# A two-network kernel on one core: head norms summed side by side on TensorE, and products reordered where stages join

## The reference

```python
def rms_norm(x, gain):
    y = x32 * lax.rsqrt(jnp.mean(x32 * x32, axis=-1, keepdims=True) + EPS)
    return (y * gain).astype(x.dtype)

def fox_attention(h, norm_g, w_in, b_f, q_gain, k_gain, w_out):
    xn = rms_norm(h, norm_g)
    q, k, v, f_logit, o_gate = jnp.split(xn @ w_in, [D, 2 * D, 3 * D, 3 * D + H], axis=-1)
    q = rms_norm(q.reshape(B, L, H, hd), q_gain) * (hd ** -0.5)
    k = rms_norm(k.reshape(B, L, H, hd), k_gain)
    ...  # softmax over q.k plus the forget sums, times v: o
    o = o * jax.nn.sigmoid(o_gate)
    return o @ w_out

# second block, the mixer's end
merged = jax.nn.sigmoid(ga) * (ya @ w_branch_sb) + jax.nn.sigmoid(gd) * (yd @ w_branch_da)
return merged @ w_out
```

## Time and profile before

| | |
|---|---|
| median of 3 runs | 1312.75 us (1312.34 to 1313.7) |
| the profiled execution's own time | 1312.96 us |
| its span, first to last instruction | 1311.3 us |
| mean granted TensorE clock | 0.999 |
| busy: PE, PEld, DVE, ACT, POOL | 99%, 96%, 73%, 48%, 5% |
| read from HBM | 250.27 MB, 192 GB/s over the span |
| share of the chain that ended last | PE 84%, DVE 7%, ACT 4%, DMA 3%, issue 2% |

### The profile page before, as it was taken

One profiled execution on the slowest core, in us unless ns is written; L12 is line 12 of the kernel. 1 busy time (PEld: TensorE's weight loads), 2 busy tenths in 40 slices (PEclk: granted clock), 3 DMA queues, 4 the chain that ended last, 5 costly groups with the idle time before them and its releaser, 6 DMA issues.

```text
span 1311.3 us, 27391 instructions
## 1 busy us (share of the span) xinstructions
PE 1295.7 (99%) x11118; PEld 1256.6 (96%) x11118; DVE 955.5 (73%) x1245; ACT 629.6 (48%) x740; POOL 62.0 (5%) x102
## 2 busy tenths in 40 slices
PE   9999999999999999999999999999999999999998
PEld 9998799999999899999999999999999899999986
DVE  7666688888567766788875788766967667877744
ACT  6365554434354345544443544443545674644433
POOL 2000000000002000000000000000011000000000
PEclk9999999999999999999999999999999999999999
DMA  8541256666745333566676587676476335476543
GB/s 290 193 156 52 103 206 204 213 194 222 240 162 207 124 121 131 208 199 204 217 242 227 179 284 263 227 242 238 152 264 208 123 138 174 162 230 221 189 164 124
DMA packets 40404, 252.30 MB, mean 192 GB/s; under 512 B 4544, under 2 KB 4800, under 8 KB 16144
## 3 DMA queue, kind: packets, MB, share of 16 engines
q1 hardware_dynamic: 29232, 211.89, 46.8%
q0 software_dynamic: 10816, 39.32, 9.5%
q10 hardware_dynamic: 288, 0.13, 0.0%
HBM read 250.27 MB, written 1.05 MB: 192 GB/s over the span
## 4 chain that ended last, share of the span: by engine, by line
PE 84%; DVE 7%; ACT 4%; DMA 3%; issue 2%; DVEq 0%; ACTq 0%; SPq 0%
PE ps L2199 68%; PE ps L2864 4%; DVE w_lo L1110 3%; ACT w_hi L486 2%; DMA raw<-in_units_mix_in 2%; DMA raw<-in_units_ffn_up 1%; PE ps L2317 1%; PE ps L2219 1%; PE ps L2548 1%; PE ps L2425 1%; PE ps L2597 1%; PE ps L2358 1%; PE ps L2651 1%; ACT scratch L697 1%; DVE proj L1550 0%
## 5 line engine op out<-in xcount | busy, mean ns | idle before, releaser
L2199 PE MATMUL ps<-x_hi,w_hi 128*128 128x258 f32 (+2 forms) x2016 | 578.2, 287 | 2.5 <-DVE x_lo L1264 1.4
L2199 PE MATMUL ps<-x_hi,w_lo 128*128 128x258 f32 (+2 forms) x2016 | 572.9, 284 | 0.0
L486 ACT ACTIVATE w_hi<-raw 128x2048 fp32r<-128x2048 f32 (+1 forms) x178 | 352.6, 1981 | 424.8 <-PE ps L2199 323.9
L2199 PE MATMUL ps<-x_lo,w_hi 128*128 128x258 f32 (+2 forms) x1856 | 527.7, 284 | 0.0
L1110 DVE TENSOR_TENSOR w_lo<-raw,w_hi 128x2048 fp32r<-128x2048 f32 (+1 forms) x178 | 422.5, 2373 | 127.5 <-ACT w_hi L486 126.4
L2199 PEld LDWEIGHTS ps<-x_hi,w_hi 128*128 128x128 f32 x2016 | 380.8, 189 | 7.0 <-DVE x_lo L1264 2.2
L2199 PEld LDWEIGHTS ps<-x_hi,w_lo 128*128 128x128 f32 x2016 | 381.2, 189 | 0.0
L2199 PEld LDWEIGHTS ps<-x_lo,w_hi 128*128 128x128 f32 x1856 | 350.4, 189 | 0.3
L2199 PE MATMUL ps<-g_hi,w_lo 128*128 128x256 f32 (+1 forms) x576 | 162.8, 283 | 0.0
L2199 PE MATMUL ps<-g_hi,w_hi 128*128 128x256 f32 (+1 forms) x576 | 162.8, 283 | 0.0
L2199 PE MATMUL ps<-g_lo,w_hi 128*128 128x256 f32 (+1 forms) x576 | 162.2, 282 | 0.0
(11 more groups left out here) (387 smaller groups left out, 1631.2 us busy)
## 6 DMA issues: line engine op xcount, KB each, us to landing
raw<-in_units_ffn_up SPq DMA_DIRECT2D x44, 1024.0 KB, 4.9
raw<-in_units_glu_up SPq DMA_DIRECT2D x44, 1024.0 KB, 5.1
v_tok<-in_w_ada_t POOLq DMA_DIRECT2D x72, 512.0 KB, 4.0
raw<-in_units_ffn_down SPq DMA_DIRECT2D x16, 1408.0 KB, 6.1
raw<-in_units_mix_in SPq DMA_DIRECT2D x20, 1024.0 KB, 5.2
raw<-in_units_hgrn_in SPq DMA_DIRECT2D x16, 1024.0 KB, 4.9
raw<-in_units_fox_in SPq DMA_DIRECT2D x14, 1024.0 KB, 4.9
raw<-in_units_glu_down SPq DMA_DIRECT2D x8, 1408.0 KB, 6.1
```

What stands on the lines that cost most here:

```text
L486: nc.scalar.activation(w_hi[s][:, 0:size], raw[s][:, 0:size], ACT.Copy).then_inc(hi_ready, 1)
L2199: ins = T_.matmul(dst, fixed, moving, start=(kt == 0 and i == 0), stop=(kt == kts - 1 and i == 2))
```

## The change

1. **Head sums.** Each of the four sums of a group has only 32 output rows now (16 equal rows for each of a tile's two heads), and the four stand side by side in bank 4. ACT takes the roots of 128 x 272. A second set of four products, each of 32 rows of its own of `head_rows` (a matrix with a one where a row stands for a head, which ACT writes once), puts the roots back on 128 rows in banks 4 to 7 (`spread_heads`), from where DVE reads them. It stands between m = 0 and m = 1 of the next v unit, and the last in the middle of the first gate half. The two v loops of PE are written out.
2. **Last norm.** ACT's roots and DVE's norm of the last group come ahead of the split of the next unit (`split_behind`); `turn_half(1)` moves ahead of `scores_of(0)`.
3. **End of the attention.** `first_out` of m = 1 is cut in two around `turn_probs(7)`, the rest of tiles 5 and 6 follows `values_of(7)`, and the last tile takes its high products ahead of its low one.
4. **Joins.** In the first unit of a `late` gemm, kt 0 to 5 of both m come first, and then kt 6 and 7 of both.
5. **Merge.** In the first mix_out unit, tiles 4 to 7 take the products with the high part first. DVE cuts the low split of the second unit into halves around `merged_lo` of tiles 6 and 7, and PE waits for the halves apart.

```diff
@@ ACT
+            for i in range(4):
+                r = slice(i * ROWS_32, (i + 1) * ROWS_32)
+                one_of_16 = ident[r, r].rearrange("p (a b) -> p a b", b=16)[:, :, 0:1]
+                ins = nc.scalar.activation(head_rows[r, :].rearrange("p (a b) -> p a b", b=HEAD), one_of_16.to_broadcast([ROWS_32, 2, HEAD]), ACT.Copy)
+            ins.then_inc(heads_set, 1)
...
             def head_rms(g):
                 act.wait_ge(hq_ss, g + 2)
-                act.wait_ge(qk_normed, g + 1)
-                steps.done(nc.scalar.activation(head_rstd, ps[:, 4:8, 0:L], ACT.Ln, bias=eps_col, scale=1.0 / HEAD))
+                steps.done(nc.scalar.activation(head_rstd, ps[:, 4, 0:L], ACT.Ln, bias=eps_col, scale=1.0 / HEAD))
...
-            gemm("fox_in", head_norms, k=1, per=2)
+            gemm("fox_in", head_norms, k=1, per=2, unroll_last=True, split_behind=True)
@@ DVE
-                    dve.wait_ge(hq_rstd, g + 2)
+                    dve.wait_ge(hq_spread, g + 1)
...
-                    V.scalar_tensor_tensor(out=proj1[:, at, :], in0=proj1[:, at, :], scalar=qk_gain[:, bass.ds(g, 1)], in1=head_rstd,
+                    V.scalar_tensor_tensor(out=proj1[:, at, :], in0=proj1[:, at, :], scalar=qk_gain[:, bass.ds(g, 1)], in1=ps[:, 4:8, 0:L],
...
             merged_lo(2, slice(4, 6))
+            dve.wait_ge(hi_ready, mix_out * 2 + 2)
+            V.tensor_tensor(w_lo[1][:, out_halves[0]], raw[1][:, out_halves[0]], w_hi[1][:, out_halves[0]].bitcast(F32), ALU.subtract).then_inc(half_lo, 1)
             merged_lo(3, slice(6, 8))
-            split_lo(mix_out, 1, UNIT)
+            V.tensor_tensor(w_lo[1][:, out_halves[1]], raw[1][:, out_halves[1]], w_hi[1][:, out_halves[1]].bitcast(F32), ALU.subtract).then_inc(lo_ready, 1)
@@ PE
                             for m in range(width // P):
+                                if first and s == 0:
+                                    column(m, range(kts - 2))
+                                    if m == 1:
+                                        column(0, range(kts - 2, kts))
+                                        column(1, range(kts - 2, kts)).then_inc(unit_done, 1)
+                                    continue
+                                ins = column(m, range(kts))
...
                 pe.wait_ge(hq_sq, g + 1)
+                pe.wait_ge(qk_normed, g + 1)
+                for i in range(4):
+                    ins = T_.matmul(ps[i * ROWS_32:(i + 1) * ROWS_32, 4, 0:L], block_ones[:, HEAD - 16:HEAD + 16], head_sq[:, i, :],
+                                    start=True, stop=True, tile_position=(0, ROWS_32 * i))
+                ins.then_inc(hq_ss, 1)
+
+            def spread_heads(g):
...
+                pe.wait_ge(heads_set, 1)
+                pe.wait_ge(hq_rstd, g + 2)
                 for i in range(4):
-                    ins = T_.matmul(ps[:, 4 + i, 0:L], block_ones, head_sq[:, i, :], start=True, stop=True)
-                ins.then_inc(hq_ss, 1)
+                    r = slice(i * ROWS_32, (i + 1) * ROWS_32)
+                    ins = T_.matmul(ps[:, 4 + i, 0:L], head_rows[r, :], head_rstd[r, :], start=True, stop=True, tile_position=(ROWS_32 * i, 0))
+                ins.then_inc(hq_spread, 1)
...
-                    first_out(1, range(6))
+                    first_out(1, range(3))
                 turn_probs(j)
...
-            first_out(0, range(5, 6))
+            first_out(1, range(3, 6))
             values_of(PAIRS - 1)
-            for kts in (range(6, 7), range(7, KD)):
+            first_out(0, range(5, 7))
+            first_out(1, range(6, 7))
+            pe.wait_ge(fox_xh, KD)
...
+            for w, x in ((hi, KD - 1), (lo, KD - 1), (hi, 2 * KD - 1)):
+                if x >= KD:
+                    pe.wait_ge(fox_xl, KD)
                 for m in range(2):
-                    ins = first_out(m, kts)
+                    ins = T_.matmul(ps[:, m, 0:L], w[:, KD - 1, m * P:(m + 1) * P], proj1_r[:, x, :], start=False, stop=x >= KD)
...
+            pe.wait_ge(merge_lo, 3)
+            out_products(range(4), (out_hi, g_hi), (out_hi, g_lo), (out_lo, g_hi))
+            for g in range(2):
+                pe.wait_ge(merge_hi, 2 + g)
+                out_products(range(4 + 2 * g, 6 + 2 * g), (out_hi, g_hi), (out_lo, g_hi))
+            for g in range(2):
+                pe.wait_ge(merge_lo, 6 + g)
+                ins = out_products(range(4 + 2 * g, 6 + 2 * g), (out_hi, g_lo))
```

More of the change, by code:

```diff
@@ L501, in gemm, with body @@
                     peel = unroll_last or last and (defer or at + 2 * pairs >= N_UNITS or UNIT_SIZE[at + 2 * pairs] != g["size"])
-                    def body(it, size, ahead=False, defer=False, split=split_hi):
+                    def body(it, size, ahead=False, defer=False, split=split_hi, split_behind=False):
                         pair = it + at // 2
@@ L507, in body @@
                                 evac(it, s2, pair)
+                            if split_behind and s2 == 1:
+                                evac(it, 2, pair)
                             if size and not (ahead and s2 == 0) and not (defer and s2 == 1):
                                 split(pair + 1, s2, size)
-                        if evac:
+                        if evac and not split_behind:
                             evac(it, 2, pair)
@@ L1129, in split_lo_half, with gemm @@
                     ins.then_inc(lo_ready, 1)
-            def gemm(name, evac=None, k=None, per=0, late=False, defer=False, ada=None, before_last=None, unroll_last=False, alone=(), split_first=False, ahead_of_last=None, halves=None):
+            def gemm(name, evac=None, k=None, per=0, late=False, defer=False, ada=None, before_last=None, unroll_last=False, alone=(), split_first=False, ahead_of_last=None, halves=None, split_behind=False):
                 g = GEMMS[name]
@@ L2173, in gemm, with unit_pair @@
                         continue
-                    def unit_pair(it, at=at, i_seg=i_seg, first=False, units=(0, 1), swap=False, behind_outer=None):
+                    def unit_pair(it, at=at, i_seg=i_seg, first=False, units=(0, 1), swap=False, behind_outer=None, half_of=None):
                         for s in units:
@@ L2187, in unit_pair, with column @@
                             T_s = T[s] if type(T) is tuple else T
[L2188 removed]
+                            def column(m, kt_range):
                                 bank, at_t = (s, m * T_s) if packed else (2 * s + m // per_bank, (m % per_bank) * T_s)
                                 dst = ps[:, bank, at_t:at_t + T_s]
[L2191 to L2193 removed]
+                                for kt in kt_range:
+                                    if in_halves and (m, kt) == (0, KD // 2):
+                                        pe.wait_ge(lo_ready, pair * 2 + (s + 3))
                                     if m == 0 and xw:
@@ L2198, in unit_pair @@
                                         fixed, moving = (x[:, kt, m * P:(m + 1) * P], w[:, kt, :]) if swap else (w[:, kt, m * P:(m + 1) * P], x[:, kt, 0:T_s])
-                                        ins = T_.matmul(dst, fixed, moving, start=(kt == 0 and i == 0), stop=(kt == kts - 1 and i == 2))
+                                        ins = T_.matmul(dst, fixed, moving, start=(kt == 0 and i == 0), stop=(kt == kts - 1 and i == 2),
+                                                        skip_group_check=first)
+                                return ins
+                            for m in range(width // P):
+                                if first and s == 0:
[5 more added lines that the diff above has]
+                                ins = column(m, range(kts))
                                 if m == width // P - 1:
```

60 lines of the change are left out of this document (33 added, 27 removed).

## The result

The changed kernel takes **1305.6 us** (median of 6 runs, 1304.4 to 1306.8) beside 1312.9 for the kernel before on the same chip (1311.7 to 1314.2); the ratio is 0.9944, 95% interval 0.9934 to 0.9953. The forecast was 1308.2 with a range of 1306.3 to 1310.7: the sign is right, but the gain of 7.3 us is 2.7 larger than the sum's 4.6, and the time lies outside the range.

What follows compares the result with a forecast made beforehand. PE's issue and pauses were taken to bound the kernel. Gains of 0.7, 0.7, 1.0, 1.55 and 0.6 made 4.6 us off the profiled 1312.96, giving 1308.4, and 1308.2 for the median; range 1306.3 to 1310.7.

Steps and rivals of the forecast that it cites:

- the sum's 4.6: Whole kernel: gains of 0.7, 0.7, 1.0, 1.55 and 0.6 us at the five places, added up.
- the reading of the bound: Whole kernel: PE, busy 1295.7 of 1311.3 us, sets the time; DVE and ACT matter only where PE waits.
- 2.1 us of issue in the HGRN scores: PE's largest wait item in the HGRN scores, 2.1 us, claimed to be left alone by the change.
- Rival (d): HGRN scores: 86 more rows of PE's program bring a third or larger issue pause, 1.0 to 2.0 us; 8%.
- (a): Head-sum spreads: 32-row tiles run one after another, 1.38 us more each, time 1313.7; 5%.
- (b): Head-sum spreads: the four 32-row products run only two at a time, 1.8 us more, time 1310.0; 11%.
- bracket plus 0.26: Price of a PE pause at a join: 0.16 us between starts and 0.10 for the first product, beyond the bracket.
- what is late next: Second units of ffn1_up and glu1_up: the low split comes late, leaving 0.40 of 1.11 and 0.45 of 0.54 us.
- Rival (c): Joins: second units of ffn1_up and glu1_up give back all gained, 0.85 us lost; with hgrn_in too, 1309.5; 12%.
- wait of 0.25: Merge: PE, there at 1090.45, waits 0.25 us for the low part of tiles 6 and 7.

Runs made afterwards that it cites:

- its loop cut four times: Kernel before with PE's ffn0_up loop cut at 3, 5, 7 and 9, same products in the same order: 1309.7 us beside 1312.1, ratio 0.9975.
- parts 1 and 2 alone: Changed kernel with the joins, the end of the attention and the merge put back as before: 1308.1 us beside 1312.1, ratio 0.9970.
- the doubled spreads: Changed kernel with each set of four spread products issued twice over: 1310.8 us, ratio 0.9989.
- with that wait moved: Changed kernel with PE's wait for the last v unit's evacuation moved behind the first gate half: 1305.05 us, ratio 0.9950.
- the one with one cut after: Changed kernel with PE's ffn0_up loop split in two, no product altered: 1307.5 us, ratio 0.9954.
- the part's own: Kernel before with only the new order of kt 6 and 7 at the joins: 1310.9 us beside 1312.7, ratio 0.9991.
- the one with the splits ahead: Changed kernel with the last fox_in pair's weight splits ahead of the last roots and norm again, on ACT and DVE: 1305.7 us, ratio 0.9947.
- with the split whole: Changed kernel with DVE's low split of mix_out's second unit whole again, behind the merge's last low part: 1305.8 us, ratio 0.9947.
- with one and two cuts: ffn0_up's loop on PE split in two on the kernel before, 1315.1 us; split in three on the changed kernel, 1312.2 us.

## Why the prediction was wrong where it was

**The sign and the reading of the bound held**: PE's own pauses and passes set the time, and the time fell.

**The step that failed** is in the first paragraph: "the largest item is 2.1 us of issue in the HGRN scores, which the change leaves alone". It doesn't change a product there, but it changes where PE's code is cut into pieces. Both pauses went, 1.38 and 1.15 us from start to start. The kernel before with its loop cut four times shows 2.4 us for that alone, and parts 1 and 2 alone gave 4.0 where their products account for 1.2. With these 2.5 added the forecast is 1305.7; measured were 1305.6. At their own places the five parts gave 4.9 in place of 4.6, so the sum was sound; but that the two times agree to 0.1 is partly luck, since in the ledger 1.8 us given back further on nearly cancel the 2.1 of waits that before's trace has and most of the others don't. Rival (d) looked at the same row and priced it in one direction only ("a third or a larger such pause"). A longer code can as well lose the pauses: with what stood at hand both directions had a claim, and the low end of the range should have been near 1305.7.

**Part 1** was right, also in its terms. Sums: 0.60 from start to start and 0.10 on either side, 0.80 as forecast. Spreads: 0.67 and the same edges, 0.87 against 0.85. Together 1.67 against the 1.83 removed, a gain of 0.17 a group. Rivals (a) and (b) fell: all four start within 0.02 us, and a pass costs 0.235. The Trainium skill's figure of 3.07 times for four row tiles (page "TensorE: Matmul & The Clock Gate", section "Measured speedup vs the span model", there for 512 columns) would make a pass 0.30, an estimate; the doubled spreads, of 272 columns, contradict it for this case. The Trainium skill's page "TensorEngine Tiling (Array Packing)" says in section "Key Properties" that a change of tiling mode drains the array; here an edge costs 0.1 us.

**Part 2** gave 0.5 in place of 0.7: 1.22 for both parts, of which 0.7 is part 1's. What was missed is the 0.3 at the first gate half: a wait that 1.83 us of sums had covered and 0.60 don't; with that wait moved, PE is 0.31 further ahead at 161 us. The prediction names such covers only for ACT and DVE. Its reason, the splits behind the roots, holds for 0.4 of the gain; the rest came with the shorter sums and roots.

**Part 3**: 1.1, with 1.0 forecast. The values start at 154.60 and the unit behind at 158.03; the gated tile (L1463) starts at 156.22 with nothing waited for, where it had a bracket of 0.45.

**Part 4**: each join gave what its bracket plus 0.26 said (0.51 against 0.50, 1.13 against 1.11, 0.55 against 0.54). The look at what is late next was right in kind: at the second unit of ffn1_up, where w_lo is waited for, 0.46 was given back here and 0.40 to 0.77 in the other kernels with the new joins, where the prediction had 0.71. So at its own places the part gave 1.8 here and 1.5 to 1.9 in those, for 1.55. Further on, up to 800 us, 1.8 more was given back in this trace, but 0.2 in the one with one cut after, nothing in the part's own and 1.9 in the one with the splits ahead; waits of that size come and go there in kernels without the new joins too. In the times the part's gain is only bounded: its own run says 1.8, with an interval on the ratio from nothing to 2.5 us. Rival (c) fell at the second units, and further on it is not excluded.

**Part 5**: 0.77 for the 0.6 forecast, and for the reason given: with the split whole, all of it is lost. The wait of 0.25 that the sum allowed for the last low part isn't in the trace.

## What to carry to other kernels

An "issue" pause in a dense run of small products can be the fetch of code, and then any edit ahead of it, even one that adds rows elsewhere, can remove or double it: price it in both directions, and compare a change also at another place of the code before its gain is believed. Number the engine's rows between such pauses; if they are a fixed count apart, shift the code (cut a loop in two) until no piece is asked for inside a dense run. When work in front of a wait gets shorter, list every wait that it covered, on the same engine too.

## What the runs showed of the hardware

- PE's code arrives in packets of 16 KB (49 packets, 0.80 MB), and PE stops at places 256 rows apart, so a row is about 64 bytes, an estimate from these two. Most packets took 0.9 to 1.3 us, and PE went on 2.2 to 2.8 us behind the packet's start in all twenty stops of eight kernels. What starts a packet stays open: they started 0 to 290 rows ahead of the stop. Before, the packets started 195 and 189 rows ahead of the stop, and the pauses were 1.38 and 1.15 us; with one and two cuts one started 0 and 12 rows ahead, and the pauses were 2.42 and 2.17. A dense run goes through 190 rows in 1.0 us; products of 0.12 each take some 11 (an estimate, 95 products).
- Places 48, 70, 82, 104, 126 and 207 cost 2.5 to 5.0 us in this stretch; 14 and 16, places worked out by arithmetic since PE doesn't stop there, cost nothing. Behind one pause of 1.97 us the granted clock was 0.58 over 4 us, and behind another of 2.22 it was 1.00.
- Four tiles of 32 rows pass in 0.235 us where the full array takes 0.229.
- Joins that hang on a weight's DMA and split differ by up to 0.95 us each between two executions of kernels that are alike there. A change under 1 us can't be read from end to end here; in the trace it can, at its own place.
